# Where the next weights are split in the corrected pairs of an up projection, and six late pieces instead of five

## The reference, cut to what matters

```python
x = layer_norm(DN_ALPHA * x + mix, ln_mix_g[l], ln_mix_b[l])      # 2048 channels
g, v = jnp.split(x @ w_up, 2, axis=-1)                            # 5632 gate and 5632 value columns
g, new_prev = causal_dwconv(g, prev, w_dw, b_dw)                  # 3 taps along time
f = (jax.nn.gelu(g, approximate=False) * v) @ w_down
x = layer_norm(DN_ALPHA * x + f, ln_ffn_g[l], ln_ffn_b[l])
```

## Time and profile before

| what | value |
|---|---|
| median of 3 runs | 2666.26 us |
| profiled execution, its span | 2667.26 us, 2665.4 us |
| PE (matmul), share of the span | 2586.7 us, 97% |
| DVE (VectorE) | 1588.1 us, 60% |
| ACT (ScalarE) | 1186.6 us, 45% |
| mean granted TensorE clock | 0.99 |

### The profile page before, as it was taken

One profiled execution on the slowest core, in us unless ns is written; L12 is line 12 of the kernel. 1 busy time (PEld: TensorE's weight loads), 2 busy tenths in 40 slices (PEclk: granted clock), 3 DMA queues, 4 the chain that ended last, 5 costly groups with the idle time before them and its releaser, 6 DMA issues.

```text
span 2665.4 us, 49128 instructions
## 1 busy us (share of the span) xinstructions
PE 2586.7 (97%) x17562; PEld 2544.3 (95%) x17562; DVE 1588.1 (60%) x2425; ACT 1186.6 (45%) x2023; POOL 219.0 (8%) x209
## 2 busy tenths in 40 slices
PE   8999799999999999999999999999999999999996
PEld 7899699999999999999998889999999999999996
DVE  7999867844443444445567886885444334444545
ACT  7777644534332334333344454554343224343333
POOL 4888100000000000000000000000000000000000
PEclk9999899999999999999999999999999999999998
DMA  7454243444444344445442213534445434444542
GB/s 274 135 135 136 73 148 136 142 151 148 159 162 151 127 148 151 145 165 165 151 167 96 95 64 119 166 133 151 153 146 169 150 131 149 147 152 148 174 146 82
DMA packets 119680, 382.52 MB, mean 144 GB/s; under 512 B 29984, under 2 KB 30368, under 8 KB 119328
## 3 DMA queue, kind: packets, MB, share of 16 engines
q1 hardware_dynamic: 99936, 373.20, 42.3%
q0 software_dynamic: 992, 6.25, 0.7%
q10 hardware_dynamic: 18688, 2.21, 0.6%
HBM read 375.32 MB, written 8.27 MB: 144 GB/s over the span
## 4 chain that ended last, share of the span: by engine, by line
PE 82%; POOL 7%; DVE 5%; issue 3%; ACT 1%; DMA 1%; POOLq 0%; DVEq 0%; SPq 0%; ACTq 0%
PE acc L396 26%; PE acc L398 26%; PE acc L397 26%; POOL prods L343 7%; DVE w_lo L1159 1%; DMA xr<-in_x 0%; DMA w_raw<-in_w_in 0%; PE pt L519 0%; PE sc L589 0%; DVE xr L1392 0%; ACT w_hi L746 0%; DVE acc L1543 0%; ACT ux L785 0%; PE sc L590 0%; DVE acc L1541 0%
## 5 line engine op out<-in xcount | busy, mean ns | idle before, releaser
L396 PE MATMUL acc<-xh,w_hi 128*128 128x320 f32 (+1 forms) x3648 | 1135.1, 311 | 17.0 <-DVE w_lo L1159 13.1
L398 PE MATMUL acc<-xh,w_lo 128*128 128x320 f32 (+1 forms) x3648 | 1132.7, 310 | 0.0
L397 PE MATMUL acc<-xl,w_hi 128*128 128x320 f32 (+1 forms) x3648 | 1128.1, 309 | 0.0
L746 ACT CAST w_hi<-w_raw 128x1024 fp32r<-128x1024 f32 (+2 forms) x680 | 705.2, 1072 | 520.8 <-PE acc L398 504.9
L1159 DVE TENSOR_TENSOR w_lo<-w_raw,w_hi 128x1024 fp32r<-128x1024 f32 (+2 forms) x680 | 842.3, 1278 | 156.0 <-ACT w_hi L746 155.9
L396 PEld LDWEIGHTS acc<-xh,w_hi 128*128 128x128 f32 x3648 | 688.2, 189 | 30.3 <-DVE w_lo L1159 18.7
L398 PEld LDWEIGHTS acc<-xh,w_lo 128*128 128x128 f32 x3648 | 689.7, 189 | 0.0
L397 PEld LDWEIGHTS acc<-xl,w_hi 128*128 128x128 f32 x3648 | 687.8, 189 | 0.6
L396 PE MATMUL acc<-h_split,w_hi 128*128 128x320 f32 x1408 | 435.3, 309 | 0.0
L397 PE MATMUL acc<-h_split,w_hi 128*128 128x320 f32 x1408 | 434.4, 309 | 0.0
L398 PE MATMUL acc<-h_split,w_lo 128*128 128x320 f32 x1408 | 434.4, 308 | 0.0
(11 more groups left out here) (224 smaller groups left out, 1848.4 us busy)
## 6 DMA issues: line engine op xcount, KB each, us to landing
w_raw<-in_up SPq DMA_DIRECT2D x352, 512.0 KB, 4.2
w_raw<-in_down SPq DMA_DIRECT2D x128, 704.0 KB, 4.9
w_raw<-in_w_in SPq DMA_DIRECT2D x64, 512.0 KB, 6.0
w_raw<-in_w_out SPq DMA_DIRECT2D x32, 512.0 KB, 4.3
w_raw<-in_w_q SPq DMA_DIRECT2D x32, 512.0 KB, 4.6
w_raw<-in_w_o SPq DMA_DIRECT2D x64, 256.0 KB, 2.8
w_raw<-in_w_kv SPq DMA_DIRECT2D x8, 512.0 KB, 4.2
out_y<-xr SPq DMA_DIRECT2D x4, 640.0 KB, 2.9
```

Source lines behind the costliest of these rows:

```text
L396: pe.matmul(out, wh, hi[:, k, 0:width], start=first, stop=False)
L397: pe.matmul(out, wh, lo[:, k, 0:width], start=False, stop=False)
L398: mm = pe.matmul(out, wl, hi[:, k, 0:width], start=False, stop=last)
L746: act.copy(w_hi[:, slot, 0:n], w_raw[:, slot, 0:n]).then_inc(hi_ready, 1)
```

## The change

On both engines the split of the next gate chunks goes to the front of a corrected pair: on ScalarE ahead of the wait for the corrected gate, on VectorE straight behind `fix_gate`. On ScalarE the casts of the next value chunks go ahead of the high part of h, and `late_affine` goes ahead of Gelu. On VectorE `late_lo` takes the piece one before (not two) and stands behind the whole body of the pair. There are six late pieces of 2, 3, 3, 3, 3 and 2 tiles. Pairs that aren't corrected keep their order.

```diff
-LATE = [(0, 3), (3, 6), (6, 9), (9, 12), (12, 16)]
+LATE = [(0, 2), (2, 5), (5, 8), (8, 11), (11, 14), (14, 16)]
 NLATE = len(LATE)
...
 # ScalarE
-                    def body(i, end, early=False, fixed=False):
-                        if early:
-                            split_next(p, i, 0, end, chunks=(0,))
+                    def body(i, end, fixed=False):
+                        if fixed:
+                            split_next(p, i, 0, end)
...
-                        split_next(p, i, 0, end, chunks=(1,) if early else (0, 1))
+                        if not fixed:
+                            split_next(p, i, 0, end)
+                        elif i:
+                            late_affine(l, i - 1)
 
                         act.wait_ge(bank_read[0], bank_count(p, i))
                         act.activation(work[:, 0, :], work[:, 0, :], ACT.Gelu).then_inc(gelu_done, 1)
+                        if fixed:
+                            split_next(p, i, 1, end)
 
                         act.wait_ge(bank_read[1], bank_count(p, i))
                         act.copy(hh[:, i, :], work[:, 1, :]).then_inc(h_hi_ready, 1)
-                        split_next(p, i, 1, end)
+                        if not fixed:
+                            split_next(p, i, 1, end)
...
                         for i in range(DEFERRED):
-                            body(i, False, early=(i == 0), fixed=True)
-                            if 0 < i <= NLATE:
-                                late_affine(l, i - 1)
+                            body(i, False, fixed=True)
...
 # VectorE
-                    def body(i, end, early=False, fixed=False):
+                    def body(i, end, fixed=False):
                         if fixed:
                             dve.wait_ge(multiplied, group_done(p, i, 0))
                             fix_gate(l, i)
-                        if early:
-                            split_next(p, i, 0, end, chunks=(0,))
+                            split_next(p, i, 0, end)
...
-                        split_next(p, i, 0, end, chunks=(1,) if early else (0, 1))
-                        if fixed and i >= 2:
-                            late_lo(l, i - 2)
+                        if not fixed:
+                            split_next(p, i, 0, end)
...
                         for i in range(DEFERRED):
-                            body(i, False, early=(i == 0), fixed=True)
+                            body(i, False, fixed=True)
+                            if i:
+                                late_lo(l, i - 1)
                             if i < NLATE:
                                 late_rows(l, i)
```

## The result

The changed kernel takes 2674.78 us (median of 9 runs, 2674.26 to 2676.14), the kernel before beside it 2667.12 us (9 runs, 2664.66 to 2669.52): a ratio of 1.0026 with a 95% interval of 1.0017 to 1.0034, 7.7 us slower. The profiled execution's span grew by 8.1 us, from 2665.4 to 2673.5.

The account below looks back on a forecast made before the run. TensorE, busy 97% of the span, bounds the kernel. 2 x (5.70 stop - 4.47 stops won + 2.3 clock) = 7.1 us on 2667.26 gives 2674.3, as a median 2673.3 us; range 2667.7 to 2678.

Parts of the forecast that it names:

- stops before: TensorE's stops ahead of pairs 4 to 7: 4.47 us a layer, 8.9 in both, all the change can win.
- stop ahead of pair 7: TensorE waits for the sixth piece's low part behind pair 6's body: 5.70 us lost a layer, a bracket of 5.44.
- slow first matmul and half clock after it: TensorE's restart after the stop: first matmul 0.10 us longer, then slower clock costing 2.3 us a layer.
- The clock: TensorE's granted clock falls to 0.5 to 0.8 for 8 us after the stop, costing 2.3 us a layer.
- The two waits on VectorE: VectorE idles for ScalarE, 0.97 us before the taps and 1.48 before the value split; removal shortens its round to 12.82.
- The edits costed at nothing: Value casts and reordering inside 1.5 us of VectorE cover, `late_affine` ahead of Gelu hidden, six pieces under half a us: price 0.
- The chain of the last low part: VectorE's work between pair 6's last matmul and TensorE's restart: `fix_value`, product, splits, low parts; sum 5.75 us.
- the formula that reads high: Time lost to the slow clock after a TensorE stop, taken as (1 - clock) x 8 us.
- The rival that the clock stays: Clock stays at 2.4 GHz at the restart ahead of pair 7, worth 4.6 us: 2668.7 us; chance 0.12.
- The other rivals: Sixth low part comes in time, 2660.8 us, chance 0.05; stops inside the pairs stay, 2682.3 us, chance 0.07.
- The last low part in time: Sixth low part in time, TensorE stands ahead of pair 7 no longer than 1.72 us: 2660.8 us; chance 0.05.
- no stops inside the pairs: Lower end of the in-time rival, TensorE without any stop: 2657.4 us; the rival's chance 0.05.

Follow-up runs that it names:

- low part ahead: Changed kernel with VectorE making the late piece's low part behind the taps, ahead of the wait for the value group: 2659.56 us.
- five pieces: Changed kernel with the five late pieces of the kernel before (3, 3, 3, 3, 4 tiles): 2657.91 us.
- clock kept: Changed kernel with 34 extra matmuls per layer on TensorE ahead of its wait for the late pieces: 2669.51 us.
- value casts alone: Kernel before with one edit: in corrected pairs ScalarE casts the next value chunks ahead of the high part of h; 2663.35 us.
- the last experiment: Changed kernel with the last low part, in pair 6 alone, ahead of VectorE's split of the next value chunks: 2667.93 us.
- the first two experiments: Changed kernel with the low part behind the taps, ahead of the value group's wait, 2659.56 us; changed kernel with five late pieces, 2657.91 us.

## Why the prediction was right

The forecast was 2673.3 us, 7.1 above before; measured, 7.7. Its steps, per layer, with a free stage of 308.26 us (low part ahead, five pieces) as the zero line:

| step | forecast us | measured us, from |
|---|---|---|
| stops before, all that could be won | 4.47 | 312.84 - 308.26 = 4.58 |
| stop ahead of pair 7, up to its first start | 5.60 | 103.07 - 97.47 = 5.60 |
| slow first matmul and half clock after it | 0.10 + 2.3 = 2.4 | 316.54 - 308.26 - 5.60 = 2.7; half clock alone, from clock kept: 316.54 - 313.98 = 2.6 |
| sum | 3.53 | 3.70 |

The prediction's 5.70 for the stop holds the 0.10 of the slow first matmul, which a difference of starts leaves to the next row. The clock was put 0.3 too low; 0.1 of that is offset by luck, since the stops before were worth 0.1 more than forecast.

**The stops before.** The two waits on VectorE were the cause, as the step said. But the prediction took 0.97 and 1.48 off together and did not ask what either is worth alone. Each alone won most of the 9.2 us: 8.4 the first, 7.0 the second. It also counted the stop ahead of pair 7 to the round. The value casts alone showed that VectorE's way through pair 6 sets that stop too: with a round short enough it stayed, as a bracket of 0.81 us.

**The edits costed at nothing** cost nothing: with `late_affine` ahead of Gelu, VectorE has no wait for Gelu in the changed kernel, as it had none before, and six pieces give the same stage as five.

**The chain of the last low part.** Forecast 5.75 us from start to start (525.12 to 530.87: 5.75). The one term with no row, 0.82 for two tiles, was measured at 0.82.

**The clock** was the size that was a little off. It was put at 2.3, between what followed a stop of 2.2 us (1.6) and one of 6.8 us (2.6), and measured 2.6. Those two rows are of other stages and were priced with the formula that reads high; why the price here isn't the 2.3 between them is not shown. The rival that the clock stays was wrong. The Trainium skill ("TensorE: Matmul & The Clock Gate", section "What's actually happening") has the throttled state as the default that activity releases; the traces agree here in all four long stops of the changed kernel and of the last experiment, and the kernel with extra matmuls kept 1.00. The stop of 2.22 us at 109.79, behind which the clock stayed at 1.00 where it fell behind one of 2.18 us at 143.20, remains unexplained: the length of a stop does not decide alone.

**The other rivals.** The last low part in time, and no stops inside the pairs, is what the first two experiments made: 2659.6 and 2657.9. It needed another place or another count, as the prediction's argument from VectorE's strict order said.

About 0.6 us of the 8.1 between the two profiled executions was there ahead of the stage (first L478 at 427.80 against 427.17) and so ahead of anything that was edited; the two stages hold 2 x 3.70 = 7.4.

## What to carry to other kernels

Where work is spread in pieces over the steps of a pipeline, the number of pieces and the place of the last one decide together: ask behind which wait the last piece stands, and whether that wait ends only when its consumer already needs the piece. A round that is a little too long costs only what it is over that of the engine that bounds the kernel, so taking out one of two waits can be worth nearly as much as both. Here a stop of TensorE of 2.8 or 5.4 us was paid a second time, with 1.4 to 2.7 us, in the clock behind it, so removing it was worth more than its length, and filling it with matmuls won that second part.

## What was not expected of the hardware

A stop of 2.77 us halved the clock as well, at 1.4 and 1.7 us, and in layer 1 only after TensorE had restarted at full speed. Runs of one unchanged stage differ: the stretch between 297 and 320 us, whose code no edit touched, was granted 0.71 in one profiled execution and 0.55 in another, and TensorE came to the edited stage 2.3 us later in the second; the kernel before ran between 2664.9 and 2672.9 us on one chip. For changes of this size the stage's own length in the trace, the same to 0.1 us in both layers for most kernels, told more than the total.
